# Paired column pages and a pooling cut in three, in a hybrid decoder step on one core

## The reference, cut to what matters

```python
mod = silu(c) @ w_ada + b_ada                       # adaLN: 6 x 1024 values a row
h = rms_norm(x, g_mix) * (1 + sc1) + sh1
z = h @ w_in                                        # 1024 x 4096: q | k | v | pool input u | 2 gates
q, k = rms_norm(q), rms_norm(k)
o = attend(q, k, v, lam)                            # differential attention; samples read a paged cache
win_sum = cs[t + 1] - cs[t + 1 - w]                 # causal pooling, w = 2, 4, 8, 16, one per group
y = (win_sum / min(pos + 1, w) - u) @ w_pool * pool_scale
merged = g0 * (o @ w_branch[:512]) + g1 * (y @ w_branch[512:])
x = x + gt1 * (merged @ w_out)
x = x + gt2 * ffn(rms_norm(x) ...)                  # layer 0 dense SwiGLU, layer 1 top-2 of 8 experts
```

## Time and profile before

| | us |
|---|---|
| median of 3 runs | 1683.52 (1680.14 to 1684.52) |
| the profiled execution's own time | 1683.85 |
| its span, first to last instruction | 1682.2 |
| PE busy | 1624.7 |
| DVE busy | 422.9 |
| ACT busy | 158.4 |

### The profile page before, as it was taken

How to read it: one execution, slowest core, us unless ns; L and a number is a source line. 1 busy time by engine, 2 the same in 40 slices (tenths; PEclk the granted TensorE clock), 3 DMA queues, 4 the chain that set the end, 5 groups by cost and what they waited for, 6 DMA issues and landing times.

```text
span 1682.2 us, 35169 instructions
## 1 busy us (share of the span) xinstructions
PE 1624.7 (97%) x15778; PEld 1018.8 (61%) x15778; DVE 422.9 (25%) x966; ACT 158.4 (9%) x410; POOL 66.6 (4%) x114
## 2 busy tenths in 40 slices
PE   6999999999999989999999999999999999999997
PEld 3778887888886878882444444444445645445454
DVE  3368343101113784432101010101010101010114
ACT  2102301000002112130100000000000000000000
POOL 3101300000000010001000000000000000000100
PEclk8999999999999999988999999999999999999999
DMA  9999978564439987427999999999999999999995
GB/s 340 365 346 321 293 252 256 152 204 143 147 111 339 300 267 200 136 55 272 397 409 404 401 408 400 407 408 395 403 393 405 403 392 402 405 393 406 407 397 194
DMA packets 275562, 535.43 MB, mean 318 GB/s; under 512 B 17837, under 2 KB 167003, under 8 KB 262610
## 3 DMA queue, kind: packets, MB, share of 16 engines
q1 hardware_dynamic: 259920, 497.12, 81.5%
q0 software_dynamic: 8608, 28.65, 5.0%
q10 hardware_dynamic: 6882, 7.37, 1.4%
HBM read 517.70 MB, written 15.82 MB: 317 GB/s over the span
## 4 chain that ended last, share of the span: by engine, by line
PE 80%; DMA 11%; DVE 4%; SPq 3%; issue 1%; another core or an unknown queue 0%; ACT 0%; DVEq 0%
PE bank L1357 29%; PE bank L1377 13%; PE bank L1050 12%; PE bank L951 9%; PE bank L1247 5%; DMA ring<-in_w_exp_gate 4%; PE bank L1223 3%; DMA ring<-in_w_exp_up 3%; PE bank L1211 2%; PE bank L959 2%; SPq L573 1%; DMA area<-in_w_exp_down 1%; DMA ring<-in_w_ada 1%; DMA area<-q_rows 1%; SPq L590 1%
## 5 line engine op out<-in xcount | busy, mean ns | idle before, releaser
L1357 PE MATMUL bank<-ring,area 128*32 128x448 f32 x3072 | 294.6, 541 | 7.2 <-issue 3.9
L1357 PE MATMUL bank<-ring,xT 128*32 128x448 f32 x3072 | 294.5, 539 | 4.8 <-issue 3.0
L463 DVE TENSOR_TENSOR area<-bank,area 128x224 f32<-128x224 f32 x96 | 54.2, 564 | 787.4 <-ACT area L907 787.3
L1050 PE MATMUL bank<-hT,ring 128*128 128x264 f32 x1024 | 242.2, 392 | 2.2 <-ACT hT L744 2.2
L1357 PEld LDWEIGHTS bank<-ring,area 128*32 128x32 f32 x3072 | 115.6, 110 | 178.6 <-issue 163.8
L1357 PEld LDWEIGHTS bank<-ring,xT 128*32 128x32 f32 x3072 | 115.1, 110 | 176.2 <-issue 167.0
L1377 PE MATMUL bank<-area 128*32 128x256 f32 x3840 | 217.7, 379 | 3.2 <-issue 2.8
L1050 PEld LDWEIGHTS bank<-hT,ring 128*128 128x128 f32 x1024 | 194.4, 192 | 39.9 <-issue 6.7
L1377 PEld LDWEIGHTS bank<-area 128*32 128x32 f32 x3840 | 138.9, 110 | 75.0 <-issue 5.1
L951 PE MATMUL bank<-hT,ring 128*128 128x264 f32 x704 | 157.4, 386 | 0.0
L951 PEld LDWEIGHTS bank<-hT,ring 128*128 128x128 f32 x704 | 133.7, 190 | 23.2 <-issue 0.4
(11 more groups left out here) (296 smaller groups left out, 901.2 us busy)
## 6 DMA issues: line engine op xcount, KB each, us to landing
ring<-in_w_exp_gate SPq DMA_DIRECT2D x256, 448.0 KB, 14.4
ring<-in_w_exp_up SPq DMA_DIRECT2D x256, 448.0 KB, 14.9
area<-in_w_exp_down SPq DMA_DIRECT2D x64, 1024.0 KB
ring<-in_w_ada SPq DMA_DIRECT2D x96, 512.0 KB, 8.4
ring<-in_w_in SPq DMA_DIRECT2D x64, 512.0 KB, 9.3
ring<-in_w_exp_down SPq DMA_DIRECT2D x32, 1024.0 KB, 15.6
area<-in_w_exp_down SPq DMA_DIRECT2D x32, 512.0 KB
ring<-in_w_ff_gate SPq DMA_DIRECT2D x22, 512.0 KB, 6.9
```

The lines of the kernel that those rows point to most:

```text
L463: dve.tensor_tensor(F["act_tok"][:, t, :].rearrange("p (i n) -> p n i", i=BODY), bank[t][:, SLICE:2 * SLICE].rearrange("p (n i) -> p n i", ...
L1050: mm = pe.matmul(bank[b][:, 0:T], w[:, c, :], hT[:, c, :], start=(c == 0), stop=(c == DC - 1))
L1357: mm = pe.matmul(bank[t][32 * g:32 * g + 32, 0:2 * SLICE].rearrange("p (s n) -> p s n", s=2), tokens[:, t, 32 * r:32 * r + 32], w[:, :, SL ...
```

## The change

Each two adjacent column pages of `w_in`, `w_branch` and `w_out` become one transfer of 1 MB into two adjacent slots: 1024 rows of 1024 contiguous bytes. SP issues it when both slots are free; PE waits for the whole pair before the first of the two. A slot of an even page of a pair counts as free only with its partner. For this the order of the stream changes: two z pages, then four adaLN pages (behind each odd i); the cached values are used four at i = 27 and four at i = 29. Z_ORDER already has adjacent columns side by side. On DVE, `pooling()` becomes `window_sums()` and `pooled_minus_own(g)`, the same instructions, and the order changes.

```diff
-            return w[:, j * P:(j + 1) * P].rearrange("(c p) n -> p c n", p=P)
+            return w[:, j * P:(j + n) * P].rearrange("(c p) n -> p c n", p=P)
...
-            return range(first + 2 * i, min(first + 2 * i + 2, last))
+            return range(first + 2 * (i - 1), min(first + 2 * (i + 1), last)) if i % 2 else range(0)
...
+            for i in range(0, ZC + GC, 2):
+                yield ("z", l, i), cols(A["w_in"][l], Z_ORDER[i], 2)
+                yield ("z", l, i + 1), None
+                for n in later_ada(l, i + 1):
                     yield ada_page(l, n)
+                if i + 1 in V_AT:
+                    for b in range(4):
+                        yield ("v", l, 4 * V_AT.index(i + 1) + b), None
+            for kind, w in (("branch", A["w_branch"]), ("out", A["w_out"])):
+                for j in range(0, 8, 2):
+                    yield (kind, l, j), cols(w[l], j, 2)
+                    yield (kind, l, j + 1), None
...
+        def freed(n):
+            return n + (2 if stream[n][0][0] in PAIRED and n % 2 == 0 else 1)
...
+                if key[0] in PAIRED:
+                    if key[2] % 2 == 0:
+                        if n >= RING:
+                            sp.wait_ge(s.pages_used, freed(n + 1 - RING))
+                        sp.dma_start(pair_cols(n % RING), src).then_inc(page_in[n % RING], 16)
+                    continue
                 if n >= RING:
-                    sp.wait_ge(s.pages_used, n - RING + 1)
+                    sp.wait_ge(s.pages_used, freed(n - RING))
...
+                if kind in PAIRED:
+                    return pair_cols(at)[:, :, (i % 2) * P:(i % 2 + 1) * P]
...
                         read_samples()
-                        pooling()
-                    if i >= 14:
-                        past_scores(i - 14)
+                    if i == 13:
+                        window_sums()
+                        pooled_minus_own(0)
+                    if i == 14:
+                        for g in range(1, H):
+                            pooled_minus_own(g)
+                    if i == 15:
+                        past_scores(0)
+                        past_scores(1)
```

More of the change, by code:

```diff
@@ L254, in run, with pair_cols @@
             return extra[:, s - RING:s - RING + n, :].rearrange("p s n -> p (s n)")
+        def pair_cols(s):
+            return ring[:, s:s + 2, :, :].rearrange("p s c n -> p (s c n)").rearrange("p (c n) -> p c n", c=DC)
         def pair(s):
@@ L286, in build @@
         Z_ORDER = tuple(range(8)) + tuple(range(12, 16)) + tuple(range(8, 12)) + tuple(range(16, 32))
-        V_FROM = 27
+        V_AT = (27, 29)
+        PAIRED = ("z", "branch", "out")
         SUM_BANK = (1, 3, 1, 7)
@@ L314, in layer_pages @@
                     yield ada_page(l, n)
-            for i, j in enumerate(Z_ORDER):
-                yield ("z", l, i), cols(A["w_in"][l], j)
-                for n in later_ada(l, i):
+            for i in range(0, ZC + GC, 2):
+                yield ("z", l, i), cols(A["w_in"][l], Z_ORDER[i], 2)
+                yield ("z", l, i + 1), None
+                for n in later_ada(l, i + 1):
                     yield ada_page(l, n)
[L319 to L325, removed]
+                if i + 1 in V_AT:
[5 more added lines that the diff above has]
+                    yield (kind, l, j + 1), None
             if l == 0:
@@ L342, in build @@
         landed, arrives = [0] * ERING, []
+        assert RING % 2 == 0
         for n, (key, _) in enumerate(stream):
-            landed[n % RING] += 16 * (PAGES if key[0] == "v" else 1)
-            arrives.append(landed[n % RING])
+            first = n - key[2] % 2 if key[0] in PAIRED else n
+            assert first % 2 == 0 or key[0] not in PAIRED
+            if first == n:
+                landed[n % RING] += 16 * (PAGES if key[0] == "v" else 1)
+            arrives.append((first % RING, landed[first % RING]))
         assert (STRAIGHT + 2 * DC) % 2 == 0
         eslot = [(STRAIGHT + i) % RING for i in range(RING)] + [RING + i for i in range(EXTRA)]
+        def freed(n):
+            return n + (2 if stream[n][0][0] in PAIRED and n % 2 == 0 else 1)
         def used_up(kind, l, i):
@@ L571, in gate_up_pages @@
                         else:
-                            sp.wait_ge(s.pages_used, STRAIGHT - RING + 2 * r + half + 1)
+                            sp.wait_ge(s.pages_used, STRAIGHT - RING + 2 * r + 2)
                         sp.dma_start(wide(at)[:, 0:WIDE],
@@ L941, in page @@
                 assert stream[n][0] == (kind, l, i)
-                pe.wait_ge(page_in[n % RING], arrives[n])
+                at, count = arrives[n]
+                pe.wait_ge(page_in[at], count)
                 used[0] += 1
+                if kind in PAIRED:
+                    return pair_cols(at)[:, :, (i % 2) * P:(i % 2 + 1) * P]
                 return slot(n % RING)
@@ L1176, in _ @@
                         output((i - 25) // 2)
-                    if V_FROM <= i < V_FROM + 4:
-                        values(2 * (i - V_FROM))
-                        values(2 * (i - V_FROM) + 1)
+                    if i in V_AT:
+                        for b in range(4):
+                            values(4 * V_AT.index(i) + b)
                     if i >= 28:
@@ L1627, in read_v, with window_sums @@
                     dve.tensor_copy(ATT["v_tok"][:, i, :], bank[i][:, :]).then_inc(s.v_out, 1)
-                def pooling():
-                    u, d = ATT["u_ext"], ATT["yT"]
-                    n = BUF + S
+                def window_sums():
+                    u, n = ATT["u_ext"], BUF + S
                     step(dve.tensor_tensor(scr_a[:, :, 1:n], u[:, :, 1:n], u[:, :, 0:n - 1], ALU.add))
@@ L1636, in pooling @@
                     step(dve.tensor_tensor(scr_b[:, 2:3, 15:n], scr_a[:, 3:4, 15:n], scr_a[:, 3:4, 7:n - 8], ALU.add))
[L1637 to L1649, removed]
@@ new lines, in pooled_minus_own @@
+                def pooled_minus_own(g):
+                    u, d = ATT["u_ext"], ATT["yT"]
+                    n, w = BUF + S, WINDOWS[g]
+                    total = (scr_a[:, 0, :], scr_b[:, 0, :], scr_a[:, 2, :], scr_b[:, 2, :])[g]
+                    step(dve.scalar_tensor_tensor(out=d[:, g, 16:S], in0=total[:, BUF + 16:n], scalar=1.0 / w,
+                                                  in1=u[:, g, BUF + 16:n], op0=ALU.mult, op1=ALU.subtract))
+                    step(dve.tensor_tensor(d[:, g, 0:16], total[:, BUF:BUF + 16], inv_count[:, g, :], ALU.mult))
+                    step(dve.tensor_tensor(d[:, g, 0:16], d[:, g, 0:16], u[:, g, BUF:BUF + 16], ALU.subtract))
+                    step(dve.tensor_tensor(d[:, g, S:T], state_sum[:, l, g, :], ATT["u_s"][:, g, :], ALU.add))
+                    r = dve.scalar_tensor_tensor(out=d[:, g, S:T], in0=d[:, g, S:T], scalar=1.0 / w,
+                                                 in1=ATT["u_s"][:, g, :], op0=ALU.mult, op1=ALU.subtract)
+                    if g < H - 1:
+                        step(r)
+                    else:
+                        r.then_inc(s.d_ready, 1)
```

2 lines of the change are left out of this document (1 added, 1 removed).

## The result

The changed kernel takes 1668.08 us (median of 5 runs, 1666.1 to 1671.83), the kernel before beside it 1684.52 us (5 runs, 1680.14 to 1685.09): a ratio of 0.9916, 95% interval 0.9902 to 0.993. Forecast was 1677.3. The medians of the same kernel so differ by 3.3 us, and the gain lies between 12 and 16 us. The profiled execution took 1671.49 us with a span of 1669.8, which is 12.4 us less than the span before.

The account below looks back on a forecast made before the run. PE, busy 1624.7 of 1682.2 us, was taken as the bound. Gains of 5.6 us in layer 1 and 0.8 in layer 0, 6.4 off 1683.85, gave 1677.4, stated as 1677.3; range 1674.5 to 1684.5.

Parts of the forecast that it names:

- Order of adaLN and of cached values: PE's page order in both layers: the same instructions in another order leave the sum as it is, 0 us.
- layer 0: Second transposes of v there start earlier because the q chain starts 1.0 us earlier: 0.8 us gained, bounds 0.3 and 1.2.
- layer 1: First transposes of v there no longer wait, the second wait 2.1 us for read_mod without clock loss: 5.6 us gained.
- the q transfers: Layer 1, with the DMA queue run dry: q's store takes 4.2 us, its read 5.7, landing at 592.7.
- the price of a pair: Transfer of two column pages, 1 MB: 3.0 us, 1.5 a page, 0.3 less than now.
- DVE's order: New order on DVE in layer 1: read_z(15) done at 594.2, before z(16) ends, so the first transposes do not wait.
- B: Layer 1: q still lands at 597.6 and PE's wait only moves to the second transposes: 1682.6 us, chance 28%.
- D: Top of layer 1: the first pair is late for z(0), losing 1 to 5.7 us; about 1680.5 us, chance 7%.
- C: Both layers: SP's longer rows delay GpSimd's q transfers, 4.2 us in layer 1, 3.2 in layer 0; 1691.6 us, chance 8%.

Follow-up runs that it names:

- e1: Kernel before with only the new order of pages, keeping single transfers and DVE's old order: 1678.91 us, ratio 0.9965 to the kernel before.
- e5: Changed kernel with adaLN pages eight at a time and all eight cached-value pages at i = 29: 1671.11 us, ratio 0.9922 to the kernel before.
- e8: Changed kernel, transfers in the new order, but PE taking one z page and two adaLN pages in turn: 1677.69 us, ratio 0.9963 to the kernel before.
- c_after: The changed kernel run again unaltered, as a control: 1671.42 us, ratio 0.9927 to the kernel before.
- e10: Changed kernel with 16 more small memsets on DVE at the head of the routing: 1672.43 us, ratio 0.9927 to the kernel before.
- e6: Changed kernel with DVE's read_mod ahead of past_scores(0) and one read_v behind each of past_scores(0) and (1): 1672.64 us, ratio 0.9933 to the kernel before.
- e9: Kernel before with 16 more small memsets on DVE at the head of the routing: 1683.6 us, ratio 0.9999 to the kernel before.
- e2: Changed kernel with DVE's old order, keeping pairs and the new page order: 1671.74 us, ratio 0.9924 to the kernel before.
- e3: Kernel before with DVE's new order alone: 1684.68 us, ratio 0.9998 to the kernel before.
- e4: Changed kernel with single transfers, keeping the new page order and DVE's new order: 1677.14 us, ratio 0.9954 to the kernel before.
- e11: Kernel with pairs, new page order and DVE's old order, plus 16 small memsets on DVE ahead of the routing: 1672.54 us, ratio 0.9919 to the kernel before.

## Why the prediction was right where it was, and wrong in its size

**The step that failed is "Order of adaLN and of cached values": "the same PE instructions in another order ... leave the sum as it is: 0".** The term measures 5.2 us in the profile (2.24 + 1.34 + 0.66 + 0.66, and 0.33 for the group in the first two pages) and e1's runs, with the 0.8 us of layer 0 in them, gained 6.0 us. It was mis-sized because a sum over instructions took their durations as fixed. A group of narrow matmuls between wide ones costs PE time beyond its own work, and the new order takes such groups away: 12 of adaLN pages and 4 of values, at 0.33 us. e5 got the same price out of twice the size (but for the values of layer 1), and e8 put the cost of the adaLN groups back, by PE's order alone. The forecast itself had two durations of a z page, 14.41 / 4 = 3.60 us in the earlier trace rows, where no adaLN page is beside it, and 3.80 in the earlier trace rows, where one follows, and used both as full speed. Part of that difference is only how rows are counted, since each row runs a little past the start of the next; by starts, a z page takes 3.56 us alone and 3.65 ahead of a group.

**Right: layer 1.** z(16) of layer 1 starts 5.59 us earlier than before. Shifted by that, the forecast's steps can be laid beside the measured ones: DVE at past_scores(0) at 588.65 + 5.59 = 594.24, forecast 594.2; second transposes at 595.83 + 5.59 = 601.42, forecast 601.4; their wait 2.13 us, forecast 2.1; no wait at the first and no fall of the clock, both as forecast. The stretch gained 5.54 us, forecast 5.6. The clock was in part luck: behind a wait of 2.0 to 2.2 us it held in the changed kernel, c_after, e5 and e8 (layer 1), and fell in e10, e6 and e8 (layer 0), at a cost of 1.6 to 1.8 us each time.

**Right in kind, off in size: the q transfers.** The quiet store took 1.9 us, not 4.2; the bound below, 3.6 us, was itself not low enough, since an adaLN page was the nearest row and the store is far smaller. The read took 5.7 us, as forecast. q landed at 584.9, in the old time 590.5 against the forecast 592.7, so DVE had it with room to spare.

**Right: the price of a pair.** The forecast took 340 to 350 GB/s and 0.3 us a page; a full stretch of pairs moves 351 GB/s. 1,048,576 bytes take 2.99 us at that rate, forecast 3.0.

**Right in number, less so in reason: layer 0.** The stretch gained 0.98 us, forecast 0.8 with bounds of 0.3 and 1.2. The reason given was that the q chain starts 1.0 us earlier. Against z(16) it starts only 0.31 us earlier (13.03 us ahead of it in the changed kernel, 12.72 before). The rest came with a store that landed in 5.03 us instead of 5.65. And e9, whose code is that of the kernel before in this place, has 9.16 us here instead of 9.70, so about half of the 0.98 can be spread.

**DVE's order** was argued as the part that lets PE reach the second transposes in time. The runs give it nothing: e2 without it is as fast. By the waits seen in e3 and e4, the reason is that read_mod stands behind past_scores and is the next thing that PE needs.

**The rivals.** B (the wait only moves) is what happens without pairs: e3's 5.4 us is its 5.6. In the seven kernels with pairs and the split the wait is 1.0 to 2.1 us; only e11, with its slow read, comes near B. D did not happen; z(0) of layer 1 waits for ACT as before:

```profile
516.26 2.02 PE L1073 MATMUL bank<-hT,ring 128*128 128x264 f32 x8 [0.82 <-ACT hT L764]
```

C (long rows hold up GpSimd's queue) said 3.2 us in layer 0. There, with full engines in every kernel, q's read took 7.43 to 7.87 us in the five kernels with single pages (mean 7.68), 7.86 to 8.06 in eight with pairs (mean 7.93), and 9.36 in e8; in layer 1 the queue had run dry, as forecast. The growth worked out from rows for this read was 0.66 x 2.8 = 1.8 us. Eight of the nine kernels with pairs show about 0.25 and one, e8, 1.7: there C's mechanism may have been at work, in one profile. The Trainium skill ("DMA: Bandwidth & Descriptors", section on queues, rings and completion order) says that each DMA engine goes round the queues packet by packet. That longer rows then make a longer turn is worked out from it and not stated there. The reads agree with it in sign, while the stores of q there, 5.15 to 5.65 us with single pages against 5.00 to 5.18 with pairs, do not.

**The time.** With 5.2 us for the groups the sum would have been 1683.85 - 6.4 - 5.2 = 1672.2 for the profiled execution, which took 1671.49; the medians of the changed kernel were 1668.08 and 1671.42. What is left of the profile is 2.5 us before the experts, told under e9, and 2.0 us back, of which 1.9 lie behind the start of the experts. That part is the same work in all kernels here and differs by that much between profiles.

## What to carry to other kernels

When you move an instruction, look at what stands on both sides of it. On PE, here, each group of narrow matmuls among wide ones had a price that no wait shows, so such groups should be few and long; PE's busy time at an unchanged count of instructions gives the price away. Fewer and longer rows for weights were worth most here to the small transfers that share the DMA engines with them, from the point at which the ring of slots is full. So ask when the ring fills, and not only whether PE waits for a page. Splitting or reordering an engine's work gained nothing where the same engine had the next thing to deliver too: e3, e4 and e6 each moved a wait to the next place.

## What the runs showed of the hardware that was not expected

- A group of 128*32 matmuls among 128*128 ones costs PE 0.33 us: 0.13 in the group itself, the rest in the 128*128 matmuls right ahead of it and behind it. No wait shows it.
- Rows of 1 KB in place of 512 B bring the full DMA engines from 289 to 351 GB/s; the experts' rows have 404.
- A 1 MB read spread over the partitions took 5.6 to 6.4 us in seven profiles with emptier engines (226 to 244 GB/s), 7.4 to 9.4 us beside full engines, and 8.6 and 10.33 us in two more stretches at 244 and 241 GB/s. Those two have no explanation here.
- Behind the same wait of 2.1 us in the same code the granted clock stayed at 1.00 in the changed kernel and fell to 0.83 (over 595 to 605 us) in e10.
- DVE stood idle for 1.9 to 4 us with nothing named that it waits for, in five of the kernels. With 16 small instructions ahead of the place it was gone in two of them, and in the kernel before that did not change the time. It was also gone with DVE's program unchanged (e4 against the changed kernel).
